# A new order of chunks, copies and masks in the mixing layers of a two-block network

## The chip, the cores and the metric

The kernel runs on one core of one Trainium2 chip. The metric is the device time of one execution in microseconds, the median of several. The core has five engines with queues of their own, which wait for one another through semaphores: TensorE (PE; PEld is its weight load), VectorE (DVE), ScalarE (ACT), GpSimd (POOL) and SyncE (SP, which here only issues DMAs).

## The reference, cut to what matters

The input is `x`, 256 tokens of 1024 numbers, batch 1. A first block of two layers (four kinds of attention, then a gated feed-forward) comes before a second block of two layers; the change lies in the second block alone, and acts in both of its layers:

```python
def second_block(x, norm1_g, w_in, ...):
    for l in range(DEPTH):                         # DEPTH = 2
        xn = rms_norm_2(x, norm1_g[l])
        x = x + mixing_sublayer(xn, w_in[l], ...)  # w_in: 1024 x 3212, w_out: 1024 x 1024
        xn = rms_norm_2(x, norm2_g[l])
        x = x + peer_ffn(xn, ...)                  # 8 heads, the best 16 of 128*128 experts each
    return x
```

The mixing sublayer has six heads of stick-breaking attention (SB: q and k normed, scores, a softplus, suffix sums over the keys, weights), six heads of an mLSTM (ML: a causal convolution of width 4 over q and k and a SiLU, an input and a forget gate per head and token, a log-sigmoid and a running sum, a running maximum m, weights exp(a_key - m_query) under a causal mask, an output gate) and four groups of a spatial gate (SG: gelu, a norm of one half, a causal 128 x 128 matrix, a product with the other half). Their outputs are normed per head, scaled and projected by w_out. The PEER feed-forward then finds for every token 8 x 16 experts (each a row of 2048 numbers in a table in memory), takes the dot product of x with the first half of each row, a gelu and a gate, and sums the second halves by these weights.

## The kernel before, in words

Tokens are in two halves of 128 (t = 0, 1). A layer of the second block is two program blocks with a barrier of all engines after each. The first runs `mixing_in` (L1191), the second `mixing_out` (L1599). On each engine the order of the work is written out by hand; semaphores make the waits.

**mixing_in** computes z = xn @ w_in in ten chunks of columns (`in_chunks`, L1174), each in eight units of 128 input numbers: unit n is chunk c = n // 8, step k = n % 8, and "(c, k)" in the text is this pair. The order before is q and k of SB (2 x 384 columns), gates and u of SG (268), three "turned" chunks for the ML convolution (256 each, made with channels on partitions), v of SG (256), SB's values (384), the output gate (384), ML's values (384). SP loads a pair of units into a ring of 8 pieces. For each unit ScalarE writes the high part of the weights (`high`, L1243 to L1249) and VectorE the low part, raw minus high (`low`, L1255 to L1259), into a ring of 8 units; TensorE then does two times three matmuls (`mm3`, L154 to L156). ScalarE's `high` of unit n waits until unit n - 8 is used. `of_pool` (L1230) gives six of the low parts, steps 3 and 7 of chunks 4 to 6, to GpSimd (`low_pool`, L1251). A chunk fills two PSUM banks, and the banks alternate by chunk; at (c, 3) ScalarE copies one bank of chunk c - 1 (`act_take`, L1261) and VectorE the other (`dve_take`, L1277), both after all eight units of it are used, and TensorE starts chunk c + 1 only then.

Between the units stand the other steps, each by its (c, k). On TensorE: `turn_if` (L1465) at (4, 4), `turn_sb` at (5, 4), `attend.sb_scores(0)` at (7, 2), `suffix_sums(0)` and `(1)` at (8, 3), `turn_cols` at (9, 2), `ml_rows(0)` at (9, 4), `ml_rows(1)` behind the last unit. On ScalarE (L1302): squares, absolute value, exponential and logarithm of the forget gate (5, 1), `sb_high`, gelu (7, 4), the sigmoid of the convolution (7, 6), magnitudes and logs of the softplus (8, 4) and (8, 6), the high part of the convolved heads (L1337) at (8, 7), the sigmoid of the output gate (9, 4), `sb_weight` (9, 6). On VectorE (L1358): the norm of q and k (4, 7) and (5, 1), the nine taps of the convolution (`taps`, L1368) at (5, 5), (6, 1) and (6, 6), `sb_low`, the running sum and maximum (7, 2) to (7, 6), the SiLU (8, 1), `scaled` (8, 2), `softplus` (L1662) at (9, 0), `sb_arg` (9, 2). GpSimd (L1439) also makes the squares of v (L1452), the low part of the convolved heads (L1458, 1536 wide) and two products for SG (L1460, L1462).

**mixing_out**. The heads are in five groups: groups 0 and 1 (three heads each) are the first half of the tokens with one block of keys a head, groups 2, 3 and 4 (two heads each) the second half with two. `ml_rows(j)` (L1729) writes for every head and block of keys the row m by a matmul with `pick` (L1745) and adds the causal mask by a matmul of the identity with `causal_big` (L1747), all in fp32. `ml_weight` takes the exponential of it, `ml_probs` multiplies by the scores. Before the change the second block starts on TensorE with `ml_scores(0)` (both first groups; L1694 is the line of every score), `sb_values(0)`, `sb_values(1)` (L1859 with the ML values), `gates()` (L1847, its matmuls L1851), `ml_values(0)`, `ml_values(1)`, scores and rows of groups 2 and 3, then `turn_y(0)` (L1882), the suffix sums and the output projection of the first half, `out(0, 0)` and `out(0, 1)`. y comes about by `y_squares` (ScalarE), `y_sums` (VectorE), the root (GpSimd, L161 to L165), `y_scaled` (VectorE, L2147 to L2156), `turn_y`, `y_high` (ScalarE, L2025), `y_low` (VectorE, L2162). w_out has high and low parts too, the last four low parts made by GpSimd (`N_LOW_DVE` = 12).

The tail treats the second half in the same way, and between its steps the first half's x is normed, turned and copied (`turn_x`, `take_x`), the queries and key scores of the first PEER head are computed, and VectorE finds the first two units' experts: `first_choice`, `second_choice`, `numbers` (L2224 to L2243; a unit is one head of one half). Its order is y_scaled(1), numbers(0), y_low(1), first_choice(1) and so on.

**The row phase**. As soon as `numbers(0)` is done, GpSimd issues gathers (L1826), 256 in a layer, each 128 rows of 8 KB, into 12 slots. The first four need nothing else; the next four wait for the third output product, the rest for the fourth and for a free slot. VectorE makes the dot products (L2259), ScalarE the gelu, VectorE a diagonal matrix (L2269), TensorE the weighted sum (L1946), and the slot is free.

## Time and profile before

| what | value |
|---|---|
| median of three runs | 2506.02 us (2505.27 to 2506.1) |
| the profiled execution | 2505.54 us |
| its span, first to last instruction | 2503.8 us |
| mean granted clock of TensorE, as a share of 2.4 GHz | 0.933 |
| TensorE busy | 2112.3 us (84%) |
| VectorE busy | 1780.1 us (71%) |
| ScalarE busy | 826.7 us (33%) |
| GpSimd busy | 709.2 us (28%) |
| the 512 gathers: bytes, share of the 16 DMA engines | 536.90 MB, 51.7% |

The page gives the span in 40 slices of 62.6 us. The DMA engines move 419 to 422 GB/s in most slices from the 16th to the 25th, and again from the 30th on: these are the row phases of the two layers. The first mixing layer lies ahead of the first of them, about 763 to 955 us from the start, the second at about 1634 to 1826 us. The shares of busy time are a mean over very different stages; the rows below are therefore taken from single stretches, in microseconds from the start of the span.

### The profile page before, as it was taken

To read this page: it belongs to the slowest core of one execution; us is meant where nothing else is said; L and a number is where in the kernel's file an instruction comes from. 1 tells how busy PE (TensorE), PEld (TensorE's weight loads), DVE (VectorE), ACT (ScalarE), POOL (GpSimd) and SP (SyncE) were. 2 spreads that over 40 slices of the span, in tenths; PEclk is the share of its full clock that TensorE was granted. 3 is DMA by queue.
4 is the path that set the end of the run, shared out by engine and by line. 5 is a ranking of instruction groups with operands and counts; after the bars stand their busy time and mean duration, and the time that the engine had idled before them with its cause. 6 is when DMAs were issued, how large, how long until landed. Compare 5 with 4: busy or idle time off the path is not lost. (4 is left out here: it accounts for less than half of the span.)

```text
span 2503.8 us, 28420 instructions
## 1 busy us (share of the span) xinstructions
PE 2112.3 (84%) x8755; PEld 1367.2 (55%) x8760; DVE 1780.1 (71%) x4243; ACT 826.7 (33%) x2026; POOL 709.2 (28%) x659
## 2 busy tenths in 40 slices
PE   8689999689997798988877777787989898877777
PEld 6459997459997685544333222276846443332232
DVE  4767775767776647778787777565586787877875
ACT  4356664456655551111111111055412111111110
POOL 0220000220002114334444444211153434444441
PEclk9799999799998878999999999998789999999999
DMA  6144433124435427999999999843189999999996
GB/s 226 68 162 152 176 134 126 67 94 151 176 134 164 135 77 291 419 421 421 421 421 421 421 422 421 349 131 121 75 334 419 421 421 421 421 421 421 421 421 273
DMA packets 138670, 700.52 MB, mean 280 GB/s; under 512 B 14393, under 2 KB 38201, under 8 KB 66873
## 3 DMA queue, kind: packets, MB, share of 16 engines
q0 software_dynamic: 73728, 536.90, 51.7%
q1 hardware_dynamic: 64824, 162.22, 18.3%
q8 instruction: 53, 0.87, 0.1%
q14 instruction: 65, 0.52, 0.1%
HBM read 698.03 MB, written 1.05 MB: 279 GB/s over the span
## 5 line engine op out<-in xcount | busy, mean ns | idle before, releaser
L1946 PE MATMUL bank<-ARENA 128*128 128x512 f32 x2048 | 990.3, 630 | 225.6 <-DVE ARENA L2269 223.4
L1946 PEld LDWEIGHTS bank<-ARENA 128*128 128x128 f32 x2048 | 384.5, 198 | 809.7 <-DVE ARENA L2269 441.6
L2259 DVE CUSTOM_DVE_ANT_0 ARENA<-ARENA 128x1024 f32<-128x1024 f32 x512 | 626.3, 1224 | 276.3 <-DMA ARENA<-in_uv_rows,ARENA 267.1
L1826 POOL DMA_INDIRECT ARENA<-in_uv_rows,ARENA x512 | 564.9, 1103 | 733.6 <-PE bank L1946 673.0
L154 PE MATMUL bank<-PARTS,PARTS 128*128 128x256 f32 (+3 forms) x1488 | 488.9, 329 | 42.5 <-DVE PARTS L1259 17.0
L155 PE MATMUL bank<-PARTS,PARTS 128*128 128x256 f32 (+6 forms) x1552 | 500.6, 324 | 0.0
L156 PE MATMUL bank<-PARTS,PARTS 128*128 128x256 f32 (+6 forms) x1552 | 499.2, 323 | 0.0
L2065 ACT ACTIVATE ARENA<-ARENA 128x1 f32<-128x1 f32 x512 | 104.0, 203 | 1047.2 <-DVE ARENA L2259 1045.2
L154 PEld LDWEIGHTS bank<-PARTS,PARTS 128*128 128x128 f32 x1488 | 287.3, 193 | 71.2 <-DVE PARTS L1259 22.1
L155 PEld LDWEIGHTS bank<-PARTS,PARTS 128*128 128x128 f32 (+2 forms) x1552 | 301.2, 195 | 18.2 <-issue 0.6
L156 PEld LDWEIGHTS bank<-PARTS,PARTS 128*128 128x128 f32 (+2 forms) x1552 | 300.4, 194 | 18.3
L2269 DVE TENSOR_SCALAR ARENA<-CON,ARENA 128x128 f32<-128x128 f32 x512 | 176.7, 345 | 9.9 <-ACT ARENA L2065 3.3
L210 POOL TENSOR_SCALAR STAT<-STAT 128x1 f32<-128x1 f32 x8 | 6.7, 834 | 459.1 <-ACT ARENA L204 459.1
L543 DVE SCALAR_TENSOR_TENSOR ARENA<-ARENA 128x255 f32<-128x255 f32 x176 | 77.5, 481 | 78.4 <-ACT ARENA L487 71.3
L1927 PE MATMUL bank<-ARENA 128*128 128x128 f32 (+1 forms) x704 | 117.3, 326 | 0.0
L1927 PEld LDWEIGHTS bank<-ARENA 128*128 128x128 f32 x704 | 107.4, 195 | 16.7 <-issue 8.6
L521 DVE TENSOR_TENSOR PARTS<-ARENA,PARTS 128x512 fp32r<-128x512 f32 x176 | 109.4, 685 | 0.0
L1259 DVE TENSOR_TENSOR PARTS<-ARENA,PARTS 128x384 fp32r<-128x384 f32 (+2 forms) x148 | 76.6, 559 | 31.9 <-ACT PARTS L1249 31.2
L465 ACT CAST PARTS<-ARENA 128x512 fp32r<-128x512 f32 x176 | 95.8, 630 | 0.0
L348 DVE TENSOR_TENSOR PARTS<-ARENA,PARTS 128x512 fp32r<-128x512 f32 (+1 forms) x112 | 65.9, 636 | 27.4 <-ACT PARTS L338 27.1
L338 ACT CAST PARTS<-ARENA 128x512 fp32r<-128x512 f32 (+1 forms) x112 | 59.0, 579 | 32.1 <-PE bank L156 26.6
L1249 ACT CAST PARTS<-ARENA 128x384 fp32r<-128x384 f32 (+2 forms) x160 | 65.1, 461 | 9.3 <-PE bank L156 7.2
(261 smaller groups left out, 2018.8 us busy)
## 6 DMA issues: line engine op xcount, KB each, us to landing
ARENA<-in_w_up_tiles SPq DMA_DIRECT2D x44, 1024.0 KB, 5.5
ARENA<-in_w_down SPq DMA_DIRECT2D x44, 512.0 KB, 3.5
ARENA<-in_w_in SPq DMA_DIRECT2D x32, 512.0 KB, 7.5
ARENA<-in_w_out SPq DMA_DIRECT2D x32, 512.0 KB, 4.8
ARENA<-in_wq_tiles SPq DMA_DIRECT2D x16, 1024.0 KB, 11.7
ARENA<-in_w_in SPq DMA_DIRECT2D x40, 384.0 KB, 3.8
ARENA<-in_w_in SPq DMA_DIRECT2D x32, 256.0 KB, 3.2
ARENA<-in_uv_rows,ARENA POOLq DMA_INDIRECT x512, 21.7
```

Source lines behind the costliest of these rows:

```text
L154: mm(out_ap, w_hi, x_hi, start=start, stop=False, skip_group_check=True)
L155: mm(out_ap, w_lo, x_hi, start=False, stop=False, skip_group_check=True)
L156: return mm(out_ap, w_hi, x_lo, start=False, stop=stop, skip_group_check=True)
L465: nc.scalar.copy(up_hi[s][u], up_raw[s][:, u, :]).then_inc(s_("up_hi"), 1)
L521: nc.vector.tensor_tensor(up_lo[s][u], up_raw[s][:, u, :], up_hi[s][u], ALU.subtract).then_inc(s_("up_lo"), 1)
L543: last = nc.vector.scalar_tensor_tensor(c[:, to], u[:, frm], w, c[:, to], ALU.mult, ALU.add)
L1826: nc.gpsimd.indirect_dma_start(out=slot[i % SLOTS], out_offset=None, in_=table[:, :], in_offset=bass.IndirectOffsetOnAxis(ap=picked[:, t, ...
L1927: last = mm(to, w[:, k, :], x, start=(k == 0), stop=(k == KD - 1), skip_group_check=True)
L1946: last = mm(row_banks[t][n][:, :], diag[i % N_DIAG], slot[i % SLOTS][:, D + n * 512:D + (n + 1) * 512], start=(c == 0), stop=(c == NPICK - ...
L2065: nc.scalar.activation(gelu_dots[:, t, c:c + 1], dots[:, t, c:c + 1], ACT.Gelu_apprx_tanh).then_inc(S("gelu_ready"), 1)
L2259: v.tensor_tensor_reduce(u, u, xn[:, t, :], 1.0, 0.0, ALU.mult, ALU.add, dots[:, t, c:c + 1]).then_inc(S("dots_ready"), 1)
L2269: v.tensor_scalar(diag[i % N_DIAG], ident, gelu_dots[:, t, c:c + 1], gate[:, t, c:c + 1], ALU.mult, ALU.mult).then_inc(S("diagonal_ready"), 1)
```

## The change

It does these things, in both layers of the second block:

- The chunks come in another order, widths as before. `of_pool` and `low_pool` go: VectorE makes all low parts, and the last four of w_out as well.
- ScalarE copies both banks of every chunk but the last, at step 7 of the next chunk; `dve_take` is left for the last chunk's second bank.
- The steps between the units stand at other places. TensorE: `turn_if` (4, 6), `turn_sb` (5, 1), `sb_scores` (6, 6), `suffix_sums` (8, 2), `turn_cols` (9, 2), gates (9, 4), `ml_rows(0)` (9, 6). ScalarE: forget gate (6, 0), `sb_high` (6, 1) to (6, 6), gelu and squares of v (7, 1), magnitudes (8, 0), logs (8, 2), the convolution's sigmoid (8, 5), the output gate (9, 0), `ml_hi` (9, 3), `sb_weight` (9, 5). VectorE: norm of q and k (4, 5) and (4, 7), forget gate (5, 6) and (6, 6), `sb_low` (7, 0) and (7, 1), running maximum (7, 2), `scaled` (7, 6), `softplus` (8, 4), v (8, 6), `sb_arg` (9, 1), SiLU (9, 2), low part of the convolved heads (9, 5). The taps are spread over single units, the first three of chunks 4, 6 and 8. GpSimd loses the squares of v (to ScalarE), the low part of the convolved heads and SG's two products (to VectorE, the latter as eight products 64 wide).
- Gates, gated product, the first groups' ML scores and `ml_weight` 0 and 1 move in ahead of the barrier; the gates write bank 0.
- `MASKS`, in bf16, holds identity, zeros and `causal_big`. `ml_rows` begins a bank with one bf16 matmul of the masks of all its heads and adds each head's row with one fp32 matmul over its blocks.
- The tail: `turn_x(0)`, `sb_values(2)` and `(3)`, `take_x(0)` and `queries(0)` come sooner, `sb_weight(4)` later; on VectorE `y_low(1)` comes ahead of `numbers(0)`.

The diff, cut to its core:

```diff
+            MASKS = arena(XN_AT + 1536, 3 * P // 2).bitcast(BF16)
-            in_chunks = [("rows", 0, 384, z[:, :, 0:384]), ("rows", 384, 384, z[:, :, 384:768]),
-                         ("rows", 2688, 268, z[:, :, ML_IF:ML_IF + 268]),
-                         ("turned", 1152, 256, 0), ("turned", 1408, 256, 2), ("turned", 1664, 256, 4),
-                         ("rows", 2956, 256, z[:, :, SG_UV + 256:SG_UV + 512]), ("rows", 768, 384, sbv),
-                         ("rows", 2304, 384, og), ("rows", 1920, 384, vaug[:, :, :, 0:HD])]
+            in_chunks = [("rows", 0, 384, z[:, :, 0:384]), ("rows", 384, 384, z[:, :, 384:768]), ("turned", 1152, 256, 0),
+                         ("rows", 2688, 268, z[:, :, ML_IF:ML_IF + 268]), ("turned", 1408, 256, 2),
+                         ("rows", 2956, 256, z[:, :, SG_UV + 256:SG_UV + 512]), ("turned", 1664, 256, 4),
+                         ("rows", 2304, 384, og), ("rows", 768, 384, sbv), ("rows", 1920, 384, vaug[:, :, :, 0:HD])]
...
-                def of_pool(n):
-                    return n // KD in (4, 5, 6) and n % KD in (3, 7)
...
                     elif kind == "rows":
-                        nc.scalar.copy(d0[:, 0, :], out_bank(c, 0)[:, 0:w]).then_inc(S("in2_taken_act"), 1)
+                        nc.scalar.copy(d0[:, 0, :], out_bank(c, 0)[:, 0:w])
+                        nc.scalar.copy(d0[:, 1, :], out_bank(c, 1)[:, 0:w]).then_inc(S("in2_taken_act"), 1)
...
                         high(act, n)
-                        if k == 3:
+                        if k == 7:
                             act_take(act, c - 1)
...
+                    act.wait_ge(S("cols_taken"), 1)
+                    attend.ml_weight(act, 0)
                     act_take(act, n_chunks - 1)
+                    attend.ml_weight(act, 1)
...
+                        if (c, k) == (2, 0):
+                            dve.wait_ge(S("consts2_loaded"), 16)
+                            nc.vector.tensor_copy(MASKS[:, 0:P], ident)
+                            nc.vector.memset(MASKS[:, P:2 * P], 0.0)
+                            nc.vector.tensor_copy(MASKS[:, 2 * P:3 * P], const("causal_big")).then_inc(S("masks_ready"), 1)
...
+                    attend.gated(dve)
+                    dve_take_last(dve)
...
                         if k == 0 and c >= 2:
                             pe.wait_ge(S("in2_taken_act"), c - 1)
-                            pe.wait_ge(S("in2_taken_dve"), c - 1)
...
                     attend.ml_rows(pe, 1)
+                    attend.ml_scores(pe, 0)
...
+                    mm(used(m_bank[j], j), MASKS[:, 0:P], masks, start=True, stop=False, skip_group_check=True)
                     for i, h in enumerate(heads):
-                        for kb in range(t + 1):
-                            mm(block(m_bank[j], j, i, kb), const("pick", (1, P), parts=NH6, off=h * P),
-                               m_row[:, t * P:(t + 1) * P], start=True, stop=(kb < t), skip_group_check=True)
-                        last = mm(block(m_bank[j], j, i, t), ident, const("causal_big"), start=False, stop=True,
+                        at = i * (t + 1) * P
+                        last = mm(m_bank[j][:, at:at + (t + 1) * P], const("pick", (1, P), parts=NH6, off=h * P),
+                                  view(m_row[:, t * P:(t + 1) * P], (0, t + 1), (1, P)), start=False, stop=(i == n - 1),
                                   skip_group_check=True)
...
+                def gates(pe):
+                    pe.wait_ge(S("uv_ready"), 1)
+                    pe.wait_ge(S("sgw_ready"), 1)
+                    pe.wait_ge(S("in2_taken_act"), 9)
...
                     sb_scores(pe, 4)
-                    ml_scores(2)
-                    ml_rows(pe, 4)
-                    turn_x(0)
-                    suffix_sums(pe, 4)
-                    queries(0)
-                    ml_scores(4)
-                    key_scores(0)
+                    ml_scores(pe, 2)
+                    turn_x(0)
+                    sb_values(2)
+                    sb_values(3)
+                    ml_rows(pe, 4)
+                    queries(0)
+                    suffix_sums(pe, 4)
+                    key_scores(0)
+                    ml_scores(pe, 4)
                     ml_values(2)
                     ml_values(3)
-                    sb_values(2)
-                    sb_values(3)
...
                     y_scaled(1)
+                    y_low(1)
                     numbers(0)
-                    y_low(1)
```

## Rows read from the trace of the kernel before

**Rows 1.** Windows: start:end, us, busy of PE, PEld, DVE, ACT, POOL, PEclk, DMA share, GB/s.
```profile
789.80:880.50 90.70, 70.23 (x452) 63.16 (x450) 60.00 (x112) 49.73 (x103) 19.52 (x15) 0.92 0.42 128
857.40:880.40 23.00, 22.74 (x104) 18.92 (x104) 7.41 (x15) 6.94 (x11) 1.15 (x1) 0.86 0.27 92
880.50:917.70 37.20, 37.00 (x175) 32.45 (x176) 21.76 (x47) 23.42 (x53) 8.96 (x6) 0.68 0.34 128
917.70:955.20 37.50, 29.40 (x204) 26.63 (x205) 19.94 (x62) 12.69 (x30) 3.67 (x3) 0.78 0.00 1
1661.90:1751.00 89.10, 68.63 (x439) 61.52 (x437) 58.92 (x110) 48.41 (x101) 19.52 (x15) 0.92 0.43 130
1100.00:1500.00 400.00, 328.07 (x753) 140.34 (x752) 315.36 (x837) 63.71 (x204) 172.78 (x157) 0.96 1.01 421
```

**Rows 2.** Waits, 789 to 881: who waited for whom, us in total, times, longest.
```profile
PE bank L1756 <- DVE ARENA L1662: 11.6, 1, 11.6
PE bank L154 <- DVE PARTS L1259: 8.5, 9, 1.9
```

**Rows 3.** Timeline of VectorE and GpSimd, 850 to 858: start, us, engine, line, operation.
```profile
850.86 0.56 DVE L1259 TENSOR_TENSOR PARTS<-ARENA,PARTS 128x384 fp32r<-128x384 f32 x1 [2.09 <-ACT PARTS L1249]
852.64 3.47 DVE L1259 TENSOR_TENSOR PARTS<-ARENA,PARTS 128x384 fp32r<-128x384 f32 x1 [1.23 <-ACT PARTS L1249]
856.04 2.94 DVE L1662 SCALAR_TENSOR_TENSOR ARENA<-ARENA 128x384 f32<-128x384 f32 x2
852.27 3.43 POOL L1458 TENSOR_TENSOR PARTS<-ARENA,PARTS 128x1536 fp32r<-128x1536 f32 x1 [4.15 <-ACT PARTS L1337]
```

**Rows 4.** Timeline of TensorE: first matmuls of chunks 1, 2, 3, and `turn_if`.
```profile
781.51 0.33 PE L154 MATMUL bank<-PARTS,PARTS 128*128 128x384 f32 x1
789.83 0.28 PE L154 MATMUL bank<-PARTS,PARTS 128*128 128x268 f32 x1
795.80 0.28 PE L154 MATMUL bank<-PARTS,PARTS 128*128 128x256 f32 x1
805.14 0.60 PE L1470 MATMUL bank<-CON,ARENA 128*6 128x128 f32 x4
```

**Rows 5.** Groups by line, TensorE, 857 to 950: busy us, mean ns, idle before.
```profile
L1745 PE MATMUL bank<-ARENA 6*128 6x128 f32 x36 | 9.6, 391 | 0.0
L1747 PE MATMUL bank<-ARENA,CON 128*128 128x128 f32 x24 | 7.4, 399 | 0.0
```

**Rows 6.** The chain that ended last, start of the second layer's second block.
```profile
1751.13 2.08 PE bank L1694 x18
1755.96 3.41 PE bank L1851 x16
```

**Rows 7.** Timeline of ScalarE: absolute value, table load, exponential of the forget gate.
```profile
806.68 0.42 ACT L1315 ACTIVATE ARENA<-ARENA 6x256 f32<-6x256 f32 x1 [2.27 <-DVE ARENA L1384]
807.15 1.28 ACT L1317 ACT_TABLE_LOAD   x1
808.45 0.42 ACT L1317 ACTIVATE ARENA<-ARENA 6x256 f32<-6x256 f32 x1
```

**Rows 8.** Timelines: value sums, root, y scaled (VectorE's last), y turned; first half.
```profile
888.71 2.77 PE L1859 MATMUL bank<-ARENA 128*128 128x65 f32 x12
895.43 2.91 POOL L165 TENSOR_TENSOR STAT<-STAT,HALF 128x16 f32<-128x16 f32 x1
900.04 0.56 DVE L2156 TENSOR_TENSOR ARENA<-ARENA 128x384 f32<-128x384 f32 x1
901.51 1.91 PE L1882 MATMUL bank<-CON,ARENA 128*128 128x128 f32 x8
```

**Rows 9.** Timelines: y scaled, its high parts, the first gather; second half.
```profile
950.42 0.56 DVE L2156 TENSOR_TENSOR ARENA<-ARENA 128x384 f32<-128x384 f32 x1
952.18 2.18 ACT L2025 ACTIVATE PARTS<-bank,GAINS 128x128 fp32r<-128x128 f32 x8 [3.91 <-PE bank L1882]
955.21 1.21 POOL L1826 DMA_INDIRECT ARENA<-in_uv_rows,ARENA  x1 [6.50 <-DVE ARENA L2243]
```

More of the change, by code:

```diff
@@ L1809, in pool @@
                     y_root(0)
-                    for n in range(N_LOW_DVE, 16):
-                        low(n)
                     x_root(0)
@@ L2279, in dve @@
                     ml_probs(1)
-                    low(0, 2)
-                    gated()
-                    low(2, 5)
+                    low(0, 5)
                     y_sums(0)
```

346 lines of the change are left out of this document (155 added, 191 removed).

## The prediction

> **What bounds the kernel now.** I read the page first for where the two layers of the second block lie, then the windows by stage, the waits, and the timelines of the engines. The row phase of a layer (256 gathers) moves 420 GB/s or so from its first gather to its end [rows 1], with the DMA engines fully taken; TensorE, busy 328 of 400 us there, is not its bound. So a layer ends a fixed stretch after its first gather, and the change, which leaves the row phase alone, is worth what it moves the first gather, twice. Ahead of that gather lie three stretches, in which the DMA share is low: the rest of the input projection (789.8 to 880.5), the first half's heads and output projection (880.5 to 917.7), and the tail to the first gather (917.7 to 955.2) [rows 1]. In the first, TensorE is busy 70.23 of 90.70 us: 20.5 us idle. The second layer has the same hole (89.10 us, 68.63 busy), so one sum serves for both. Who made it wait: once 11.6 us for the softplus of L1662, and nine times, 8.5 us in all, for a low part of VectorE (L1259) [rows 2].
>
> Why the softplus was late is in [rows 3]: a low part takes VectorE 0.56 us at 850.86 and 3.47 us at 852.64, while GpSimd forms the low part of the convolved heads from 852.27 for 3.43 us; the two softpluses behind it then take 2.94 us together, with GpSimd still at its next two products. Both engines read from SBUF and one stands still. Before that, ScalarE reached the logarithms only after stalling at each fourth unit of a chunk on "all of the last chunk is used".
>
> **The change, part by part, for one layer.**
>
> *Input projection.* The work of TensorE is nearly the same. A chunk of 384 columns takes 8.32 us (781.51 to 789.83), one of 268 takes 5.97, a unit of 256 columns 0.718 (thirteen from 795.80 to 805.14) [rows 4]. The new order of chunks has the same widths, so it costs nothing itself.
> - Idle: the 20.5 us go, and with ten gaps 0.16 us each that idle time doesn't show, since a gap is counted from the modelled end of a matmul, 0.28 us after its start, where the next would start after 0.12 [rows 4]: 1.6 us.
> - Clock: after the long hole the mean granted clock of 857.4 to 880.4 is 0.86 [rows 1], so 0.28 of 23 us at 1.2 GHz instead of 2.4, half of which is lost: 3.2 us.
> - Masks: 24 fp32 records of the masks (L1747, two a matmul) are 7.4 us and the 36 of the picks (L1745) 9.6 us in all five groups [rows 5]. Five bf16 matmuls of 384 or 512 columns replace the masks. Bounds for one: a float32r matmul of 256 columns every 0.12 us [rows 4], and the 0.62 of an fp32 mask of 128 columns. I take 0.26 (1.3 in all), near the first, since these are wider than 256 but far from the fp32 row, so 6.1 saved, and 1.8 for picks that are merged in pairs (an estimate: the 24 records of the two-block groups become half as many, each twice as wide, with a fixed part of 0.15 us saved on twelve). Together 7.9: 3.1 here, 3.1 in the second stretch, 1.7 in the tail. Forming the masks is three small VectorE writes among the second chunk's units, where it waits for work.
> - Moved in ahead of the barrier: the first two groups' ML scores (L1694, 2.1 us) and the gates (L1851, 3.4 us) [rows 6]. They ran at 1.2 GHz there (the stretch after 880.5 has 0.68 [rows 1]); at 2.4 I take 1.3 and 1.7: 3.0, with 5.5 as the other bound. Their partner on VectorE is four products, on ScalarE the six exponentials of `ml_weight`.
> - New idle. VectorE carries back six low parts, the 1536-wide low part and the gated products, and loses its copies of banks (now ScalarE's) and all waits for GpSimd: its 60.0 of 90.7 us [rows 1] become some 55 of 70. ScalarE's 49.7 become some 57. No engine is above TensorE, but in-order waits remain. ScalarE's takes now stand at a chunk's last unit, where its ring is full anyway, so TensorE has eight units in hand instead of four. Walking the queues on with these durations I find TensorE late at: the first scores after unit (6,6), whose `sb_low` stand behind two low parts and behind ScalarE's logarithm chain (2.9 us, with all units of chunk 7 queued behind it); the taps of chunk 4 (0.5); the suffix sums (0.6, instead of 11.6); unit (9,4) behind the 1536-wide copy (1.1); and the gates, which wait for ScalarE's take of chunk 8 (1.5, with units 77 to 79 and both mask groups behind them). Sum 6.6. Bounds: nothing, and all of the old 20.1 [rows 2]; I take 6.6 because it is near the 8.5 of the old small waits.
> - Sum: -20.5 -1.6 -3.2 -3.1 +3.0 +6.6 = **-18.8 us**.
>
> ScalarE's two logarithm chains hold four table loads on this path. In [rows 7] a load follows the work before it at 0.05 us, takes 1.28 us, and the exponential starts 0.02 us after its end (807.15 + 1.28 = 808.43 against 808.45). The Trainium skill, "ScalarE: Activation LUTs", section "What ACT_TABLE_LOAD costs", states a drain of 1.38 us on top of each load. No such time stands between these rows. By that page the new idle would be about 5.5 us longer per layer; by the rows it isn't.
>
> *First half's heads.* ML scores and gates have left (2.1 and 3.4 us), masks save 3.1: TensorE stands before the turning of y 8.6 us sooner. But the chain to y is longer: value sums end at 891.48, GpSimd's root ends at 898.34, and y is scaled at 900.60 [rows 8], 9.1 us later. The value sums end 5.5 us sooner, so y is ready at 895.1 of the old count, and TensorE, which was the late one (901.51), gains 901.5 - 895.1 = 6.4, less 0.2 for the hand-over: **-6.2 us**; 2.4 of the 8.6 turn into a wait for y. VectorE takes back the last four low parts of w_out (some 0.7 each, by the 0.56 of 384 columns [rows 3]) behind y_low, while the first half of the output product runs: nothing; without that cover, 2.8.
>
> *Tail.* Moving turn_x, its copies, the first queries and sb_values ahead lets the value sums of the other half end sooner: the 1.7 us of masks, and 0.6 of the 8.1 us that TensorE is idle in this stretch (37.50 less 29.40 [rows 1]; the bounds are nothing and all, and most of it is the wait for y, which stays): -2.3. Against it stands the new order on VectorE: y_low(1) now comes before numbers(0). Today the heads are scaled at 950.98 and the gather starts at 955.21, 4.2 us on; ScalarE's high parts run 952.18 to 954.36 in that time [rows 9]. y_low can't end before about 1.1 us after the last of them, 955.5, so the numbers start 4.5 us later: +4.5. The output product starts some 3 us sooner for it, but the first four gathers don't wait for it. Sum: **+2.2 us**. SP's queue gets its releases sooner, and the loads of w_out and wq have over 10 us before their first use; nothing.
>
> Per layer -18.8 - 6.2 + 2.2 = -22.8. The clock may fall again after the new 2.9 us gap or in the thin work at the end; the bound is 0 to 3.2 (above), I take 1.0 as the gap is a quarter of the old one. That is -21.8, for two layers -43.6. The profiled execution took 2505.54 us (span 2503.8), 0.5 under the median of 2506.02. So 2505.5 - 43.6 = 2461.9, on the median's footing 2462.
>
> **The rivals.**
> 1. *VectorE becomes the bound* of chunks 4 to 8. For: the small waits of today are all for it. Against: 60.0 of 90.7 us busy, part of it standing still. It decides if new idle passes 13 us: 6 or more us less per layer, 2474; the range's end at the full 20 us of idle is 2489.
> 2. *The order on VectorE outweighs the rest, slower.* Its place is y_low(1) ahead of numbers(0), its price 4.5 us per layer, and it decides where the first two stretches give under 2.3 us, that is where a chain (logarithms, convolution, gates) still ends the projection at 880. With nothing gained upstream: 2506 + 9 = 2515. Against: the 11.6 us hole has a cause that is taken out.
> 3. *Clock stays full and the waits don't come* : new idle under 3 us, y's wait shorter: 26 to 28 per layer, 2452.
> 4. *Table loads hold ScalarE longer* than the 1.28 of the rows: another 1.28 on four loads is 5.1 per layer, 2472. The rows leave no room for it [rows 7]. It is the rule of "ScalarE: Activation LUTs" in the Trainium skill, as told above.
> 5. *The row phase isn't led by the first gather*, so that it ends where it does: 2506. Against: [rows 1].
>
> **How the numbers follow.** My case 0.60, rival 1 0.17, rival 3 0.13, rival 4 0.02, rival 5 0.03, rival 2 0.05. Its own range would be 2453 to 2470. To hold eight in ten it must reach into rivals 1 and 3: 2447 to 2483. Differences under 0.2% (5 us) can't be told from none here. Faster: 0.92; within 0.2%: 0.03; slower: 0.05.
>
> **What would show it.** In the waits of the new profile the 11.6 us for the softplus is gone; GpSimd has no 1536-wide product, and no low part on VectorE lasts over 1 us in chunks 7 to 9; the first block ends about 70 us after the second chunk instead of 90; TensorE has its longest wait at the first scores (3 us) and some 2 us before the turning of y. From y scaled to the first gather it is 8.7 us instead of 4.2; first gathers stand at about 933 and 1782. I'd be wrong if the projection still ends past 875, or if the row phase, at 420 GB/s, doesn't start as much sooner as its first gather.

## The result and the profile after

| what | before | after |
|---|---|---|
| median | 2505.64 us (2504.68 to 2506.1, four runs) | 2464.72 us (2463.2 to 2466.11, four runs) |
| ratio, 95% interval | | 0.9837 (0.982 to 0.9854) |
| profiled execution, its span | 2505.54, 2503.8 us | 2466.03, 2464.0 us |
| mean granted clock | 0.933 | 0.932 |

The forecast of 2462 was 2.7 us too low, on a gain of 41. Of all executions in this document two, one of e1 (3368 us, granted clock 0.56) and one of e10 (6884 us, 0.29), were far slower than the others, and the medians leave them out. In the traces the two first gathers came 19.6 and 39.7 us sooner (935.59 instead of 955.21, 1785.86 instead of 1825.56), and the end 39.8. So the row phases kept their length, as [rows 1] had said: they hold at 421 GB/s in the last window row below. The windows of the profile after, by stage, in the columns of [rows 1]: input projection, first half's heads and output product, tail to the first gather; the projection of the second layer, from its third chunk on like the first row; 400 us of row phase.

```profile
789.80:861.50 71.70, 67.42 (x476) 63.95 (x474) 53.28 (x118) 54.78 (x117) 8.69 (x5) 0.98 0.53 162
861.50:892.30 30.80, 28.99 (x127) 23.15 (x127) 21.28 (x46) 21.87 (x47) 3.10 (x2) 0.72 0.40 154
892.30:935.60 43.30, 37.56 (x211) 33.61 (x211) 22.08 (x71) 12.69 (x30) 3.67 (x4) 0.72 0.00 1
1641.60:1714.30 72.70, 68.70 (x476) 65.34 (x474) 53.29 (x118) 54.71 (x118) 8.70 (x5) 0.95 0.53 160
1080.00:1480.00 400.00, 331.67 (x753) 144.03 (x752) 315.98 (x837) 64.22 (x204) 180.74 (x157) 0.94 1.01 421
```

The projection is 19 us shorter with TensorE busy 2.8 us less: most of what left is idle time, 4.3 us where there were 20.5. VectorE's busy time fell by 6.7 us although it got all the low parts back; its copies of banks had gone to ScalarE, which is busy 5.1 us more. In the second layer the stretch from the third chunk to the second block is 72.8 us instead of 90.8. The waits of TensorE, 789 to 868, which answer to [rows 2]:

```profile
PE bank L1670 <- DVE PARTS L1284: 2.5, 1, 2.5
PE bank L1763 <- ACT ARENA L1252: 1.0, 1, 1.0
PE bank L154 <- DVE PARTS L1241: 0.7, 2, 0.4
PE bank L1850 <- PEq L2315: 0.5, 1, 0.5
```

The 11.6 us for the softplus is gone, and of nine waits for a low part two are left. The longest is the first scores' (L1670) for the low part of q and k (L1284), then the gates' (L1763) for ScalarE's copy of a bank; the last row is the barrier. The timelines of VectorE around the softplus (L1638) and the wide low part of the convolved heads (L1417), against [rows 3]:

```profile
836.68 1.03 DVE L1241 TENSOR_TENSOR PARTS<-ARENA,PARTS 128x384 fp32r<-128x384 f32 x2
837.62 1.02 DVE L1638 SCALAR_TENSOR_TENSOR ARENA<-ARENA 128x384 f32<-128x384 f32 x2
850.87 1.75 DVE L1417 TENSOR_TENSOR PARTS<-ARENA,PARTS 128x1536 fp32r<-128x1536 f32 x1
```

Two softpluses take 1.02 us instead of 2.94, and VectorE makes the low part in 1.75 us for which GpSimd took 3.43. The masks, as one group by shape (TensorE, 831 to 927), against [rows 5]:

```profile
L1725 PE MATMUL bank<-ARENA 6*128 6x256 f32 x12 | 6.2, 668 | 0.0
L1725 PE MATMUL bank<-ARENA 6*128 6x128 f32 x12 | 1.9, 287 | 0.0
L1722 PE MATMUL bank<-ARENA 128*128 128x512 bf16 x3 | 1.8, 616 | 0.0
L1722 PE MATMUL bank<-ARENA 128*128 128x384 bf16 x2 | 0.7, 338 | 0.0
```

Masks and picks were 7.4 + 9.6 us and are 2.5 + 8.1. The end of the tail is in the timelines of VectorE, ScalarE and GpSimd, against [rows 9]: y scaled, its high parts, its low parts, the last instruction of the numbers, the first gather.

```profile
926.70 0.56 DVE L2123 TENSOR_TENSOR ARENA<-ARENA 128x384 f32<-128x384 f32 x1
928.02 2.17 ACT L2002 ACTIVATE PARTS<-bank,GAINS 128x128 fp32r<-128x128 f32 x8 [2.39 <-PE bank L1873]
929.19 2.16 DVE L2129 SCALAR_TENSOR_TENSOR PARTS<-bank,GAINS,PARTS 128x128 fp32r<-128x128 f32 x8 [1.93 <-ACT PARTS L2002]
934.39 0.23 DVE L2210 TENSOR_SCALAR ARENA<-ARENA 128x16 uint32<-128x16 f32 x1
935.59 1.21 POOL L1838 DMA_INDIRECT ARENA<-in_uv_rows,ARENA  x1 [10.59 <-DVE ARENA L2210]
```

From y scaled (927.26) to the gather it is 8.3 us, where it was 4.2: the numbers now wait behind the low parts.

### The profile page after: what moved, and what is told of

Same layout as the page of the kernel before. It is cut to its first block and busy times, and to the rows that moved or that the text cites. A ratio compares the mean times of both kernels' runs of the same rounds, so it can differ in the third digit from the quotient of the medians.

```text
span 2464.0 us, 28188 instructions
## 1 busy us (share of the span) xinstructions
PE 2103.0 (85%) x8693; PEld 1360.9 (55%) x8698; DVE 1769.3 (72%) x4263; ACT 837.5 (34%) x2050; POOL 692.9 (28%) x631
## 5 line engine op out<-in xcount | busy, mean ns | idle before, releaser
L1934 PEld LDWEIGHTS bank<-ARENA 128*128 128x128 f32 x2048 | 390.7, 201 | 811.7 <-DVE ARENA L2236 429.4
L1838 POOL DMA_INDIRECT ARENA<-in_uv_rows,ARENA x512 | 582.0, 1137 | 724.1 <-PE bank L1934 652.4
L154 PE MATMUL bank<-PARTS,PARTS 128*128 128x256 f32 (+4 forms) x1488 | 488.6, 328 | 25.5 <-DVE PARTS L275 8.6
L155 PEld LDWEIGHTS bank<-PARTS,PARTS 128*128 128x128 f32 (+2 forms) x1552 | 302.2, 195 | 17.9
L1915 PEld LDWEIGHTS bank<-ARENA 128*128 128x128 f32 x704 | 111.3, 203 | 17.7 <-issue 9.9
L348 DVE TENSOR_TENSOR PARTS<-ARENA,PARTS 128x512 fp32r<-128x512 f32 (+1 forms) x112 | 65.9, 636 | 26.9 <-ACT PARTS L338 26.2
L1237 ACT CAST PARTS<-ARENA 128x384 fp32r<-128x384 f32 (+2 forms) x160 | 68.9, 460 | 36.2 <-PE bank L156 33.3
L338 ACT CAST PARTS<-ARENA 128x512 fp32r<-128x512 f32 (+1 forms) x112 | 59.0, 580 | 31.5 <-PE bank L156 26.7
## 6 DMA issues: line engine op xcount, KB each, us to landing
ARENA<-in_wq_tiles SPq DMA_DIRECT2D x16, 1024.0 KB, 11.6
```

What stands on the lines that cost most here:

```text
L154: mm(out_ap, w_hi, x_hi, start=start, stop=False, skip_group_check=True)
L155: mm(out_ap, w_lo, x_hi, start=False, stop=False, skip_group_check=True)
L1838: nc.gpsimd.indirect_dma_start(out=slot[i % SLOTS], out_offset=None, in_=table[:, :], in_offset=bass.IndirectOffsetOnAxis(ap=picked[:, t, ...
L1915: last = mm(to, w[:, k, :], x, start=(k == 0), stop=(k == KD - 1), skip_group_check=True)
L1934: last = mm(row_banks[t][n][:, :], diag[i % N_DIAG], slot[i % SLOTS][:, D + n * 512:D + (n + 1) * 512], start=(c == 0), stop=(c == NPICK - ...
```

## The experiments

Each kernel was timed beside the kernel before, whose medians lie between 2504.8 and 2506.4 us, so the ratios can be set side by side. The table holds what the traces show in the first of the two layers: when the second block's first matmul starts, when TensorE begins to turn y of the first half, when the first half's output product ends, when y of the second half is scaled, and the first gather. "Tail" is from the end of the output product to y scaled, in the first and in the second layer. In the kernel before, e4 and e10 the gates and the first ML scores stand behind the start of the second block, in the others ahead of it, so that column compares only kernels of one kind.

| run | us | block 2 | y turned | product ends | y scaled | gather | tail |
|---|---|---|---|---|---|---|---|
| before | 2505.6 | 880.7 | 901.5 | 917.6 | 951.0 | 955.2 | 33.3, 33.4 |
| after | 2464.7 | 862.0 | 875.1 | 892.4 | 927.3 | 935.6 | 34.9, 34.6 |
| e1_numbers_first | 2458.0 | 860.5 | 873.5 | 890.9 | 925.8 | 930.0 | 34.9, 34.9 |
| e2_old_tail | 2460.5 | 862.1 | 874.1 | 890.4 | 923.0 | 931.8 | 32.7, 31.5 |
| e3_both | 2452.7 | 863.7 | 878.2 | 894.5 | 927.2 | 931.4 | 32.6, 35.1 |
| e4_before_ml_lo_vector | 2491.1 | 874.2 | 893.4 | 909.6 | 943.0 | 947.2 | 33.3, 33.4 |
| e5_softplus_old_steps | 2480.4 | 868.7 | 883.3 | 899.6 | 934.0 | 942.4 | 34.5, 34.9 |
| e6_fp32_masks | 2479.5 | 865.7 | 881.1 | 897.4 | 933.9 | 942.2 | 36.5, 36.5 |
| e7_takes_at_3 | 2472.7 | 866.6 | 880.0 | 896.9 | 932.2 | 940.7 | 35.3, 30.2 |
| e8_values_in_gap | 2453.7 | 860.1 | 872.2 | 888.4 | 919.9 | 924.1 | 31.5, 31.5 |
| e9_ml_lo_on_gpsimd | 2473.2 | 866.4 | 880.9 | 897.3 | 931.9 | 940.2 | 34.6, 34.5 |
| e10_gates_behind_barrier | 2467.1 | 855.6 | 873.7 | 890.5 | 920.8 | 929.6 | 30.2, 34.9 |
| e11_scores_and_gates_later | 2442.2 | 861.8 | 873.9 | 890.5 | 922.2 | 926.4 | 31.7, 28.4 |
| e12_filled_wait | 2444.2 | 859.1 | 871.2 | 888.0 | 916.4 | 920.7 | 28.4, 30.1 |

### The tail: two edits, alone and together

e1, on VectorE:

```diff
                     y_scaled(1)
-                    y_low(1)
                     numbers(0)
+                    y_low(1)
```

> The changed kernel with numbers(0) put back ahead of y_low(1) on VectorE, nothing else. My theory: the row phase is led by the first gather, which in the changed kernel follows the scaling of y by 8.3 us instead of 4.2, so this undoing makes each layer 4.1 us shorter: 2465 - 8 = 2456.5 us, first gather at about 931.5. Rival: the output product that y_low(1) feeds is what the row phase waits for (its fifth gather waits for the third product): then it is the same or slower, 2465 to 2469.

e2, on TensorE (and the same on VectorE and ScalarE for `take_x` and `sb_weight(4)`):

```diff
                     ml_scores(pe, 2)
-                    turn_x(0)
-                    sb_values(2)
-                    sb_values(3)
                     ml_rows(pe, 4)
-                    queries(0)
+                    turn_x(0)
                     suffix_sums(pe, 4)
-                    key_scores(0)
+                    queries(0)
                     ml_scores(pe, 4)
+                    key_scores(0)
                     ml_values(2)
                     ml_values(3)
+                    sb_values(2)
+                    sb_values(3)
```

> The changed kernel with the tail's order on TensorE, ScalarE and VectorE (turn_x, sb_values 2 and 3, ml_rows 4, queries 0, suffix sums 4, take_x, softplus 4, sb_weight 4) as before the change; y_low(1) still ahead of numbers(0). My theory: the new order puts y(1) 34.9 us behind the end of the first half's product where it was 33.3, and it hides the 1.7 us of masks, so the old order gives 33.3 - 1.7 = 31.6: 3.3 us per layer, 2465 - 6.6 = 2458. Rival: the order is worth what it was made for and the lost time is TensorE's clock, which falls either way: the same within 2 us, 2463 to 2468.

e3 is both.

> Both undone: the old tail's order and numbers(0) ahead of y_low(1). If both theories hold the two add up, 2465 - 8 - 6.6 = 2450 us. If the output product ends the row phase's start, what the first gives is lost when the second is there: 2456 to 2460.

Measured: e1 2457.97 us, ratio 0.9809 (0.979 to 0.9829); e2 2460.49, 0.9818 (0.9802 to 0.9835); e3 2452.68, 0.9783 (0.9766 to 0.9799). The numbers first are worth 3.4 us a layer in the medians, and in the trace the step from y scaled to the gather is 4.2 us again, as before the change (the last numbers and the gather, VectorE and GpSimd of e1):

```profile
928.84 0.23 DVE L2210 TENSOR_SCALAR ARENA<-ARENA 128x16 uint32<-128x16 f32 x1
928.98 2.16 DVE L2129 SCALAR_TENSOR_TENSOR PARTS<-bank,GAINS,PARTS 128x128 fp32r<-128x128 f32 x8
930.03 1.21 POOL L1838 DMA_INDIRECT ARENA<-in_uv_rows,ARENA  x1 [6.50 <-DVE ARENA L2210]
```

The two edits add up (6.8 and 4.2 us alone, 12.0 together), so the output product, which e1 delays, does not lead the row phase. The old order of the tail seemed worth 2 us a layer too, of the 3.3 expected. The tails of the table then showed that this reading was too quick; it is taken up under the clock below.

### The hole before the suffix sums: contention or order

e4 is the kernel before, with the low part of the convolved heads taken from GpSimd and given to VectorE at (9, 6):

```diff
+                        if (c, k) == (9, 6):
+                            dve.wait_ge(S("ml_high"), 1)
+                            tt(ml_lo, qkm, ml_hi, ALU.subtract).then_inc(S("ml_low"), 1)
...
-                    pool.wait_ge(S("ml_high"), 1)
-                    nc.gpsimd.tensor_tensor(ml_lo, qkm, ml_hi, ALU.subtract).then_inc(S("ml_low"), 1)
```

> The kernel before the change, with one thing moved: the low part of the convolved heads (1536 wide) is made by VectorE at (9, 6) instead of GpSimd beside the softplus. As the prediction put it, VectorE and GpSimd stood still for each other, and the hole of 11.6 us ahead of the suffix sums came from that: the hole falls to some 7.5 us or less and the time by 4 us or more per layer, 2505.6 - 8 = 2497. Rival: the hole is one of order (the softplus stands behind the low part of unit 72, whose high part stands behind the logarithms and the 1536-wide copy), and GpSimd only fills it: the hole stays over 9.5 us, 2502 to 2506.

Measured 2491.13 us, 0.9944 (0.9928 to 0.9961). The waits of TensorE in the projection, then VectorE's low part and softpluses, then the window from 789.8 to 0.2 us before the second block, where that of [rows 1] ends too:

```profile
PE bank L154 <- DVE PARTS L1259: 8.5, 9, 1.9
PE bank L1757 <- DVE ARENA L1663: 7.8, 1, 7.8
```

```profile
851.47 0.56 DVE L1259 TENSOR_TENSOR PARTS<-ARENA,PARTS 128x384 fp32r<-128x384 f32 x1 [1.15 <-ACT PARTS L1249]
851.95 1.02 DVE L1663 SCALAR_TENSOR_TENSOR ARENA<-ARENA 128x384 f32<-128x384 f32 x2
```

```profile
789.80:874.00 84.20, 67.56 (x443) 60.91 (x441) 56.33 (x112) 48.80 (x101) 16.20 (x14) 0.96 0.45 138
```

Against [rows 1 to 3]: the low part is 0.56 us again and the softpluses 1.02, and the hole falls from 11.6 to 7.8. So the contention made 3.8 us of it; the 7.8 that are left have another cause, and e5 tries the place of the steps for it. The window is 6.5 us shorter: 3.8 of the hole, and 2.7 of TensorE's own busy time (70.23 to 67.56), with its granted clock at 0.96 instead of 0.92. In all it is 7.3 us a layer, where I had expected 4 or more.

e5 is the other half of the question, the changed kernel with the softplus chain at its old steps:

```diff
-                        if (c, k) == (8, 0):
+                        if (c, k) == (8, 4):
                             attend.magnitudes(act, 0, 1)
-                        if (c, k) == (8, 2):
+                        if (c, k) == (8, 6):
                             attend.logs(act, 0, 1)
-                        if (c, k) == (8, 5):
+                        if (c, k) == (8, 3):
                             act.wait_ge(S("ml_conv_ready"), 1)
...
-                        if (c, k) == (7, 6):
+                        if (c, k) == (8, 3):
                             attend.scaled(dve, 0)
...
-                        if (c, k) == (8, 4):
+                        if (c, k) == (9, 0):
                             attend.softplus(dve, 0)
```

> The changed kernel with the softplus chain at its old steps alone: scaled (8,3), sigmoid of the convolution (8,3), magnitudes (8,4), logs (8,6), softplus (9,0); GpSimd still has no wide product. My theory: after the run with ml_lo on VectorE, 7.8 of the 11.6 us hole were the order of the steps, so it comes back here, less what the deeper lookahead saves: a wait of 5 to 7 us for the softplus ahead of the suffix sums, some 6 to 7 us per layer, 2477 us. Rival, GpSimd's contention was the whole of it: a wait under 1 us, 2465 to 2468.

Measured 2480.42 us, 0.9902 (0.9886 to 0.9919): 15.7 us, 7.9 a layer. The wait is there (TensorE's waits; then the suffix sums in its timeline):

```profile
PE bank L1735 <- DVE ARENA L1638: 5.5, 1, 5.5
```

```profile
844.03 2.93 PE L1735 MATMUL bank<-ARENA,CON 128*128 128x384 f32 x4 [5.52 <-DVE ARENA L1638]
```

The order alone brings back 5.5 us of hole, and the second block starts 6.8 us later. The four suffix sums run 2.93 us after the gap instead of 1.45, at half the clock. That was the theory, with a price of 7.9 us a layer where 6 to 7 were expected.

e9 puts only the low part of the convolved heads back on GpSimd, in the new order:

```diff
-                            dve.wait_ge(S("ml_high"), 1)
-                            tt(ml_lo, qkm, ml_hi, ALU.subtract).then_inc(S("ml_low"), 1)
...
+                    pool.wait_ge(S("ml_high"), 1)
+                    nc.gpsimd.tensor_tensor(ml_lo, qkm, ml_hi, ALU.subtract).then_inc(S("ml_low"), 1)
```

> The changed kernel with the 1536-wide low part of the convolved heads back on GpSimd (it starts when the high part is there, at unit (9,3) of ScalarE). Theory, contention: the low part of VectorE beside it takes about 3.5 us instead of 0.56 again; VectorE is ahead of TensorE by a few units there, and it saves the 1.6 us of doing the wide one itself, so TensorE loses 0 to 2 us a layer: 2465 to 2469. If the low part stalls as in the run before the change and TensorE is only two units ahead: 3 us a layer, 2471. Rival, it helps since VectorE is relieved: 2461 to 2463.

Measured 2473.18 us, 0.9876 (0.9859 to 0.9892): 8.5 us, more than any of the three cases gave. VectorE and GpSimd in its timelines, and TensorE's waits:

```profile
850.36 4.44 DVE L1241 TENSOR_TENSOR PARTS<-ARENA,PARTS 128x384 fp32r<-128x384 f32 x3 [1.49 <-ACT PARTS L1237]
```

```profile
849.99 3.45 POOL L1440 TENSOR_TENSOR PARTS<-ARENA,PARTS 128x1536 fp32r<-128x1536 f32 x1 [18.51 <-ACT PARTS L1326]
```

```profile
PE bank L154 <- DVE PARTS L1241: 3.5, 3, 2.8
```

Three low parts take 4.44 us beside GpSimd's product, where two take 1.03 and one 0.55 without it: 2.9 us lost, and TensorE, which is hardly ahead there, waits 2.8 us more. The second block starts 4.4 us later; the rest of that is its lower clock (0.94 to the end of the projection, 0.98 in the changed kernel).

### Masks and copies

e6 writes the masks in fp32 and one pick a block, as before:

```diff
-                    mm(used(m_bank[j], j), MASKS[:, 0:P], masks, start=True, stop=False, skip_group_check=True)
...
+                        for kb in range(t + 1):
+                            mm(block(m_bank[j], j, i, kb), const("pick", (1, P), parts=NH6, off=h * P),
+                               m_row[:, t * P:(t + 1) * P], start=True, stop=(kb < t), skip_group_check=True)
+                        last = mm(block(m_bank[j], j, i, t), ident, const("causal_big"), start=False, stop=True,
```

> The changed kernel with ml_rows as before (fp32 masks, picks one block at a time). My sum gave the masks and picks 7.9 us per layer: 3.1 + 3.1 on the path in the projection and the first half's heads, 1.7 in the tail. But in the heads of the first half 2 us of it are covered by the wait for y. So +5.5 to +6 per layer, 2476 us. Rival, most of it lies beside waits: +3 per layer, 2471; if the matmuls were all on the path, +7.9, 2480.

Measured 2479.45 us, 0.9897 (0.988 to 0.9913): 14.7 us, 7.4 a layer, nearly the whole of the 7.9 of the sum, and between the two highest cases, 2476 and 2480. By its groups (TensorE, 835 to 936) masks and picks take 17.9 us, where the changed kernel has 10.6 in the groups shown above:

```profile
L1720 PE MATMUL bank<-ARENA 6*128 6x128 f32 x36 | 10.2, 411 | 0.0
L1722 PE MATMUL bank<-ARENA,CON 128*128 128x128 f32 x24 | 7.7, 414 | 0.0
```

By the table the second block starts 3.8 us later, the product ends 5.0 later and y of the second half is scaled 6.7 later. I had expected the wait for y to cover 2 us. That wait (1.3 us) is indeed gone, but y itself comes 5.2 us later: 3.8 by the later start, and 1.4 since the stretch up to it takes 14.5 us instead of 13.0, at a granted clock of 0.50 instead of 0.56.

e7 takes the banks at step 3:

```diff
-                        if k == 7:
+                        if k == 3:
                             act_take(act, c - 1)
```

> The changed kernel with ScalarE's copies of the banks at step 3 of the next chunk instead of step 7. My prediction said that TensorE has eight units in hand instead of four by this. Theory: ScalarE stalls at every fourth unit again and TensorE gets back part of the 8.5 us of small waits, 2 to 5 us per layer: 2469 to 2475. Rival, the place doesn't matter since ScalarE has room: within 1 us per layer, 2465.

Measured 2472.73 us, 0.9871 (0.9855 to 0.9887): 8 us, 4 a layer. TensorE's waits in the projection:

```profile
PE bank L1670 <- DVE PARTS L1284: 2.5, 1, 2.5
PE bank L154 <- DVE PARTS L1241: 2.0, 7, 0.4
PE bank L1735 <- DVE ARENA L1638: 1.1, 1, 1.1
```

Seven small waits are back instead of two, and one for the softplus. Idle time is only 1.4 us more in sum (that of the gates is gone), the second block 4.6 us later; the clock is 0.96 there instead of 0.98. The lookahead is worth 4 us a layer, within the 2 to 5 expected, but the waits hold 1.4 us of it; the lower clock stands beside the rest, and how much of it is the clock's is not shown.

e10 brings gates, gated product, the first groups' ML scores and `ml_weight` behind the barrier again:

```diff
-                        if (c, k) == (9, 4):
-                            attend.gates(pe)
...
-                    attend.ml_scores(pe, 0)
...
+                    ml_scores(pe, 0)
                     sb_values(0)
                     sb_values(1)
+                    gates(pe)
```

> The changed kernel with the gates, the gated product, the ML scores and ml_weight of the first two groups behind the barrier, as before the change, all else as changed. My sum: the move costs the projection 3.0 us and takes 2.1 + 3.4 us out of the first half's heads, so undoing it is +2.5 us of TensorE's time per layer, and the exponentials of ml_weight come back on the way to the value sums: 2470 us. Rival, the move was worth the whole 5.5 us: 2476. Rival, all of it is covered by the wait for y: 2464 to 2466.

Measured 2463.05, 2467.09 and 2473.5 us, with a ratio of 0.9862 (0.9843 to 0.9882). The median lies between the 2470 expected and the 2464 to 2466 of the rival, the single times span both, and the interval meets that of the changed kernel (0.982 to 0.9854). In the profiled run y was turned 1.3 us sooner than in the changed kernel in the first layer; counted from the gather of the first layer, it was turned 2.1 us later in the second. What the move is worth stays unsettled: 1.2 us a layer by the medians, -1.3 and 2.1 by the two layers of the trace.

### Better versions, and the clock

e8 is e3 with the SB values in the gap of the tail:

```diff
                     turn_x(0)
+                    sb_values(2)
+                    sb_values(3)
                     suffix_sums(pe, 4)
...
                     ml_values(3)
-                    sb_values(2)
-                    sb_values(3)
```

> The run with both tail edits (numbers first, old order of the tail), and the SB values of groups 2 and 3 between the turning of x and the suffix sums of group 4, where TensorE waited 1.7 us for the softplus. Theory: the 32 matmuls (some 3.6 of the 5.5 us of 48 for both kinds at full clock) fill that wait and the value sums of the second half end 1.7 us sooner: first gather 1.7 us sooner per layer, 2449.3 us against 2452.7. Rival: they are later than the softplus, the suffix sums start 2 us later and nothing is gained: 2452 to 2454.

Measured 2453.7 us (2447.17 to 2455.76), 0.9797 (0.9781 to 0.9813): no better than e3, whose ratio was 0.9783. The profiled run was the fastest of them, and its tails are 31.5 us. As a median the edit gives nothing.

e11 is e8 with two steps of TensorE later in the projection:

```diff
-                        if (c, k) == (6, 6):
+                        if (c, k) == (7, 1):
                             attend.sb_scores(pe, 0)
...
-                        if (c, k) == (9, 4):
+                        if (c, k) == (9, 5):
                             attend.gates(pe)
```

> The run with the SB values in the gap, with the first SB scores at unit (7,1) instead of (6,6) and the gates at (9,5) instead of (9,4). TensorE waits 2.5 us and 1.0 us for them there; three units later (2.2 us) and one later (0.9 us) little of it is left. Theory: 2 to 3 us a layer sooner, 2448 to 2450 us against 2453.7. Rival: the later scores delay the softplus and a wait of 2 us stands at the suffix sums instead, or y's chain is behind: 2453 to 2456.

Measured 2442.21 us (2437.98 to 2446.47), 0.9749 (0.9731 to 0.9768): the best of all, 22.5 us under the changed kernel. The gain over e8 was more than the 5 us a run or so that I had expected, and it isn't where I had put it: the second block starts at 861.8, no sooner than in e8 (860.1), since the waits for the scores and the gates turned into others:

```profile
PE bank L154 <- DVE PARTS L1241: 2.3, 4, 0.9
PE bank L1735 <- DVE ARENA L1638: 1.2, 1, 1.2
```

In the second layer its tail is the shortest, 28.4 us. The profiled run of e8 was 6.5 us under that kernel's median, so the two traces differ by 4.3 us only, and their largest differences lie in stretches that the edit didn't touch: in the second layer y is turned 12.1 us after the second block's start instead of 14.5, at a granted clock of 0.76 instead of 0.50, and the tail is 3.1 us shorter at 0.94 instead of 0.84. Why the median fell by 11.5 us stays open; it is not shown that the waits did it.

Here the clock has to be read. e7 and the changed kernel have the same instructions in the tail, and e7's own two layers differ by 5 us in it. The windows of both tails of e7, then those of e10, which has them in the other order, both of the changed kernel, both of e3 (the old order of the tail with the new masks) and one of the kernel before:

```profile
896.90:932.20 35.30, 30.49 (x188) 28.01 (x187) 16.18 (x49) 10.52 (x22) 3.67 (x3) 0.76 0.00 0
1750.40:1780.60 30.20, 24.24 (x187) 22.27 (x187) 16.18 (x49) 10.62 (x22) 3.66 (x3) 0.92 0.01 1
```

```profile
890.50:920.80 30.30, 24.29 (x188) 22.32 (x187) 16.19 (x49) 10.64 (x22) 3.66 (x3) 0.92 0.00 1
1739.90:1774.80 34.90, 30.46 (x187) 27.98 (x187) 16.19 (x49) 10.54 (x22) 3.66 (x3) 0.76 0.00 1
```

```profile
892.30:927.30 35.00, 30.51 (x188) 28.02 (x187) 16.20 (x49) 10.51 (x22) 3.66 (x3) 0.76 0.00 0
1743.08:1777.66 34.58, 28.75 (x187) 26.27 (x187) 16.19 (x49) 10.62 (x22) 3.66 (x3) 0.80 0.00 1
```

```profile
894.54:927.19 32.65, 26.47 (x188) 23.94 (x187) 16.20 (x51) 10.51 (x22) 3.66 (x3) 0.83 0.00 1
1737.35:1772.42 35.07, 29.86 (x187) 27.33 (x187) 16.20 (x51) 10.41 (x22) 3.66 (x3) 0.76 0.00 1
```

```profile
1788.10:1821.50 33.40, 26.91 (x195) 24.58 (x194) 16.23 (x51) 10.51 (x22) 3.67 (x3) 0.82 0.00 1
```

VectorE, ScalarE and GpSimd are busy for the same 16.2, 10.5 and 3.7 us or so in each; in the new order TensorE needs 24.3 us at a granted clock of 0.92 and 30.5 at 0.76 for the same 188 instructions or so. The last row is the kernel before, at 0.82 in both of its tails, with the dearer masks.

Of the twelve tails in the new order with the new masks (after, e1, e5, e7, e9, e10) six ran at 0.76 (34.9 to 35.3 us), four at 0.80 (34.5 to 34.6) and two at 0.92 (30.2). Of the four tails of e2 and e3, with the old order and the new masks, one ran at 0.76 and took 35.1 us, no less than the new order does there; the others, at 0.83 to 0.86, took 31.5 to 32.7. So at the same low clock the two orders take the same time, and what the old one gained (2.1 us a layer in e2, 2.6 in e3 over e1) goes with a higher clock in three of its four tails. Whether the order brings that clock, or chance did, isn't shown by four tails.

e12 tried to hold the clock up by filling TensorE's wait for y with eight matmuls that nobody reads:

```diff
                     ml_rows(pe, 3)
+                    pe.wait_ge(S("ml_probs"), 2)
+                    for _ in range(8):
+                        mm(bank[0][:, 0:3 * P], MASKS[:, 0:P], MASKS[:, 0:3 * P], start=True, stop=True)
                     turn_y(0)
```

> The run with the later scores and gates, and eight bf16 matmuls of 384 columns between the rows of group 3 and the turning of y, whose result nothing reads: TensorE works on in the 1.3 to 5 us in which it waits for y. By the masks each is 0.16 us at 2.4 GHz and 0.3 at 1.2, so they take 1.3 to 2.5 us and delay y's turning by at most 1.2 where the wait is short. What the traces show: one tail takes 30.2 us at a granted clock of 0.92 and 35.3 at 0.76 in the same run, so the clock is worth 5 us there. Theory: the idle time ahead of the output product is what lets the clock fall later; then the tail runs at 0.92 or more in most cases, 3 us a layer: 2436 to 2439 us against 2442.2, with the spread of the runs smaller. Rival: the fall comes from elsewhere, the clock in the tail is 0.76 to 0.94 as before, and nothing or up to 1 us a layer is lost: 2442 to 2444.

Measured 2444.21 us (2438.35 to 2446.04), 0.9755 (0.974 to 0.977): the rival. The wait for y fell from 4.0 and 4.2 us to 1.7 and 1.8, y came no later after the second block's start, the times spread as in e11, and the median is not lower. The profiled run, the fastest of five, has its tails at 0.94 and 0.87, which says little beside e11's 0.84 and 0.94. The stronger row is e7's: in both layers the wait for y is 1.3 us and the first half's output product runs at 0.86, and the tail behind it runs at 0.76 in one and at 0.92 in the other. So this idle time alone does not decide; what does stays open.

## Why the prediction was right, and which term was off

**What bounds it.** Right. The end moved by 39.8 us, the second first gather by 39.7, with 421 GB/s between. Nothing of the gain was given back in the row phases.

**Input projection, -18.8.** Measured 880.70 to 861.97, less 0.3 by which its first chunk started later: -19.0 in the first layer. From the third chunk on, where the prediction's stretch began, it is -18.8 (90.9 to 72.1 us) there and -18.0 in the second layer. That the first is the forecast to the tenth is luck, since terms were off both ways. The new idle was put at 6.6 us and is 4.3: the wait for the scores 2.5 (2.9 forecast), the gates 1.0 (1.5), and the taps, the suffix sums and unit (9, 4) together 0.7 instead of 2.2. Against these 2.3 us stands the clock, 0.98 and not 1: by the prediction's own working 1.4 us of 71.7 (an estimate: 0.04 of the stretch at half the clock, half of it lost). The prediction's [rows 3] blamed the hole on contention. That was half the story: e4 gives 3.8 of 11.6 us to it, and e5 brings 5.5 us back by order alone. The sum didn't suffer, since the change does both, but rival 2's "the 11.6 us hole has a cause that is taken out" rested on two causes. Without the new places 7.8 of the 11.6 us would have stayed with the old lookahead (e4), 5.5 with the new one (e5). The masks (7.9 for all three stretches) measured 7.4 in e6, but by TensorE's busy time, 17.0 to 10.6 us, it is 6.4: a bf16 mask matmul took 0.34 to 0.62 us instead of the 0.26 put for it, and the picks fell by 1.5 instead of 1.8. The "fixed part of 0.15 us" behind that 1.8 no run shows; a merged pick of 256 columns took 0.67 us, a single one 0.29 to 0.39.

**Table loads.** The changed kernel's rows again show a load of 1.28 us and the activation behind it 0.01 later (ScalarE, the logarithms of the softplus):

```profile
834.01 1.28 ACT L1657 ACT_TABLE_LOAD   x1
835.30 0.94 ACT L1657 ACTIVATE ARENA<-ARENA 128x384 f32<-128x384 f32 x2
```

The drain of 1.38 us on top, by "ScalarE: Activation LUTs" of the Trainium skill, section "What ACT_TABLE_LOAD costs", doesn't show here either, and rival 4 didn't come.

**First half's heads, -6.2.** Measured 36.94 to 30.38: -6.6 in the first layer, and 36.98 to 28.62, -8.4, in the second. The wait for y is there; instead of 2.4 us it is 1.34 in the first layer (TensorE's timeline) and 3.94 in the second, where TensorE did the work ahead of it at a granted clock of 0.74 instead of 0.56:

```profile
875.07 1.97 PE L1873 MATMUL bank<-CON,ARENA 128*128 128x128 f32 x8 [1.34 <-DVE ARENA L2123]
```

The low parts of w_out show no wait of TensorE in that stretch, as said. Only e10 tried this stretch by itself, and it didn't settle it.

**Tail, +2.2.** Measured 37.6 to 43.2 us: +5.7, and +5.3 in the second layer. Of its two parts the numbers behind y_low were +4.5 and measured +4.1 (8.3 less 4.2), and e1 takes them out again. The mis-sized term is the other, "-2.3", the value sums that end sooner: it measured +1.6 in the first layer and +1.2 in the second. The cheaper masks are there (e6's two tails, without them, are 36.5 us, 1.6 and 1.9 longer, at a granted clock of 0.72), and TensorE's idle time fell. Its busy time should have fallen by the masks' 1.7 us, and rose from 26.9 to 30.5 and 28.8: the term was worked out at the 0.82 of the tail before, and the changed kernel's tails had 0.76 and 0.80. Between 0.76 and 0.92 lie 5.1 us in e7, and where such a tail ran at 0.92 it was 3.1 us shorter than before, near the term. "The clock may fall again" with its bound of 0 to 3.2 and its 1.0 looked at one gap only; the tail alone can take 5. The order put one wait in the place of another: TensorE waits 1.6 us for the normed x (L1892 for L2147), since `turn_x` stands ahead of the rows that covered it, where in the old order (e3) it waits 0.2 for x and 1.7 for the softplus. In the order of e8 the first is 0.2 or less and the second is gone.

**Sum.** -19.0 - 6.6 + 5.7 is -19.9 for the first layer against -21.8; in the second it is 187.6 to 169.4 us from the first matmul to the gather, -18.3, and 1.8 came in the stretch between. The second layer has its own reason to be short of the forecast: -18.0 - 8.4 + 5.3 would be -21.1, but the first two chunks took 19.5 us instead of 16.8, at a granted clock of 0.84 instead of 1.00, and no term stood for that. In all the traces show 39.8 us against the 43.6 of the sum: the tail missed its term by over 3 us a layer, and the first half's heads gave 0.4 and 2.2 us more than theirs. The rivals: VectorE didn't become the bound (53.3 of 71.7 us), the order on VectorE cost its 4 us and outweighed nothing, and rival 3 asked for new idle under 3 us where it is 4.3. The new order of the chunks and the new places of the taps were never undone alone.

## What to carry to other kernels

A hole behind a late step may have several causes that each cover the other: take them out one at a time (e4, e5) before giving the whole hole to the one that the timeline shows. Every step on the queue ahead of the value that starts the longest phase is paid nearly in full, here 3 to 4 us a layer for eight low parts that could wait. Where TensorE's granted clock moves in short stretches, give each stretch its own range by rows at both levels, and read both layers of a trace before a few microseconds are put down to an order: two layers of one run differed by 5 us with the same instructions.

## What the runs showed of the hardware that I hadn't expected

- The granted clock of a stretch isn't fixed by its program: the tail of the same kernel had 0.76 in one layer and 0.92 in the next (e7), and the reverse in e10. In both of e7's tails TensorE had run its output product without a gap, then scores of 64 rows, with the same wait of 1.6 us for the normed x, so none of these tells the two apart. Filling an earlier wait (e12) left the median where it was. What sets it is open.
- GpSimd's product doesn't only take time from VectorE while it runs; its price for TensorE was larger than the stall: 2.9 us of VectorE's time stood behind 4.4 us by the start of the second block (e9), with the clock at 0.94 instead of 0.98.
- An edit of two steps moved the median by more than all the waits that it went for (e11: 11.5 us where 7 were waited for in both layers together, and others came in their place), and one trace of each kernel doesn't show why.
